# Regrouping results with VectorE blocks and on-chip transfers instead of TensorE transposes, in a two-layer encoder trunk

## The reference

```python
h = x                                            # (1, 256, 2048)
for i in range(2):
    u = rmsnorm(h, norm_mix[i])
    if i == 0:   # mixer A
        val, gate = split(u @ w_pw1 + b_pw1)     # 2048 -> 4096
        v = causal_depthwise_conv(val * sigmoid(gate), w_dw) + b_dw     # 31 taps
        m = silu(rmsnorm(v, g_norm)) @ w_pw2 + b_pw2
    else:        # mixer B
        gate_b, gate_c, v = split(u @ w_in)      # 2048 -> 6144
        m = (gate_b * causal_depthwise_conv(gate_c * v, w_conv3)) @ w_out
    h = h + m
    h = h + square(relu(rmsnorm(h, norm_mlp[i]) @ w1)) @ w2             # 2048 -> 8192 -> 2048
    h = h + sigmoid(rmsnorm(h, norm_ple[i]) @ w_gate) * (p[i] @ w_proj)
return rmsnorm(h, norm_final)
```

## Time and profile before

| what | value |
|---|---|
| median of three runs | 2347.74 us |
| profiled execution | 2345.66 us, span 2343.9 us |
| TensorE busy | 2317.7 us, 99% of the span |
| VectorE busy | 1407.9 us, 60% |
| ScalarE busy | 1000.7 us, 43% |
| transfers | 431.59 MB, mean 184 GB/s |
| the SP queue's packets | 54.9% of 16 engines' time |
| granted TensorE clock, mean | 0.998 |

### The profile page before, as it was taken

How to read it: one execution, slowest core, us unless ns; L and a number is a source line. 1 busy time by engine, 2 the same in 40 slices (tenths; PEclk the granted TensorE clock), 3 DMA queues, 4 the chain that set the end, 5 groups by cost and what they waited for, 6 DMA issues and landing times.

```text
span 2343.9 us, 31333 instructions
## 1 busy us (share of the span) xinstructions
PE 2317.7 (99%) x11258; PEld 1958.1 (84%) x11258; DVE 1407.9 (60%) x1761; ACT 1000.7 (43%) x1160; POOL 1.6 (0%) x9
## 2 busy tenths in 40 slices
PE   8999999999999999999999999999999999999997
PEld 6888678888888888888888888888888888888886
DVE  5999956555555555555656565556556556556565
ACT  2000445434444444455644444554344344344554
POOL 0000000000000000000000000000000000000000
PEclk9999999999999999999999999999999999999999
DMA  9444155555555555555555555555555555565553
GB/s 298 151 153 154 67 187 189 181 197 190 187 197 185 191 197 183 193 179 180 188 201 185 188 188 183 185 189 190 191 193 186 192 195 182 194 195 182 196 197 108
DMA packets 231282, 431.59 MB, mean 184 GB/s; under 512 B 7181, under 2 KB 40461, under 8 KB 230413
## 3 DMA queue, kind: packets, MB, share of 16 engines
q1 hardware_dynamic: 230448, 428.90, 54.9%
q10 hardware_dynamic: 632, 0.89, 0.1%
q0 software_dynamic: 144, 1.05, 0.1%
HBM read 428.70 MB, written 2.10 MB: 184 GB/s over the span
## 4 chain that ended last, share of the span: by engine, by line
PE 86%; issue 13%; DVE 0%; ACT 0%; DMA 0%; POOL 0%; DVEq 0%; POOLq 0%; ACTq 0%
PE acc L384 20%; PE acc L356 18%; PE acc L358 18%; PE acc L357 18%; PE acc L387 10%; PE acc L346 1%; PE acc L531 0%; PE acc L532 0%; PE acc L533 0%; DMA work<-in_cf_b_pw 0%; DVE wlo L820 0%; ACT L800 0%; DVE res L895 0%; DVE work L890 0%; DVE h L898 0%
## 5 line engine op out<-in xcount | busy, mean ns | idle before, releaser
L820 DVE TENSOR_TENSOR wlo<-raw,whi 128x1024 fp32r<-128x1024 f32 x732 | 885.9, 1223 | 726.0 <-ACT whi L552 717.4
L552 ACT ACTIVATE whi<-raw 128x1024 fp32r<-128x1024 f32 x732 | 769.8, 1059 | 853.9 <-PE acc L358 530.8
L356 PE MATMUL acc<-whi,both_b 128*128 128x512 f32 x1120 | 438.7, 392 | 1.9 <-DVE wlo L820 1.9
L358 PE MATMUL acc<-whi,both_b 128*128 128x512 f32 x1120 | 436.6, 390 | 0.0
L357 PE MATMUL acc<-wlo,both_b 128*128 128x512 f32 x1120 | 436.4, 390 | 0.0
L356 PE MATMUL acc<-whi,both_a 128*128 128x512 f32 x768 | 299.7, 390 | 0.0
L358 PE MATMUL acc<-whi,both_a 128*128 128x512 f32 x768 | 298.9, 389 | 0.0
L357 PE MATMUL acc<-wlo,both_a 128*128 128x512 f32 x768 | 298.9, 389 | 0.0
L384 PE MATMUL acc<-both_b,whi 128*128 128x512 f32 x1024 | 257.3, 392 | 0.0
L384 PE MATMUL acc<-both_a,whi 128*128 128x512 f32 x1024 | 257.3, 392 | 0.0
L356 PEld LDWEIGHTS acc<-whi,both_b 128*128 128x128 f32 x1120 | 210.7, 188 | 46.6 <-issue 2.6
(11 more groups left out here) (137 smaller groups left out, 1305.3 us busy)
## 6 DMA issues: line engine op xcount, KB each, us to landing
raw<-in_mlp_w SPq DMA_DIRECT2D x256, 1024.0 KB, 5.1
raw<-in_sc_w_in SPq DMA_DIRECT2D x48, 1024.0 KB, 5.2
raw<-in_cf_w_pw SPq DMA_DIRECT2D x64, 512.0 KB, 8.6
raw<-in_ple_w_gate SPq DMA_DIRECT2D x32, 1024.0 KB, 5.0
raw<-in_cf_w_pw SPq DMA_DIRECT2D x16, 1024.0 KB, 5.0
raw<-in_sc_w_out SPq DMA_DIRECT2D x16, 1024.0 KB, 5.0
wproj<-in_ple_w_proj SPq DMA_DIRECT2D x2, 2048.0 KB, 14.0
h<-in_x SPq DMA_DIRECT2D x4, 512.0 KB, 9.3
```

Source lines behind the costliest of these rows:

```text
L356: nc.tensor.matmul(o, xhi[:, k, s], hi, start=first and c == 0, stop=False)
L358: mm = nc.tensor.matmul(o, xlo[:, k, s], hi, start=False, stop=last and c == 1)
L552: nc.scalar.activation(whi[:, e % SLOTS, :, :], raw[:, e // 2, 2 * (e % 2):2 * (e % 2) + 2, :], ACT.Copy).then_inc(hi_ready, 1)
L820: nc.vector.tensor_tensor(wlo[:, e % SLOTS, :, :], raw[:, e // 2, 2 * (e % 2):2 * (e % 2) + 2, :], whi[:, e % SLOTS, :, :].bitcast(F32), A ...
```

## The change

1. **Turning.** The result `res` is turned by one VectorE instruction (`turn`, new) that transposes every 32 x 32 block by itself, into `turned`. The blocks then have to change partitions: SP issues 16 transfers (`move`, new), each from 32 partitions to 32 partitions, 32 KB in runs of 128 bytes, into `xt`. `operand_hi`, `operand_lo`, `to_vpad` and `short_out` read `xt` (in SBUF) and no longer PSUM. TensorE has no transposes left after the front.
2. **The MLP's up blocks** are computed by `multiply`, as all others are: the residual operand is held still, the weights are streamed. Their results come token by partition and so need turning too. ACT applies ReLU with the norm factor and the square; the down blocks' results are added without a factor. `NORM_MLP` becomes a full inverse root.
3. **Order.** `turn` and `add_gated` stand before DVE's split step e = 3. `move` stands in SP's list behind the first tile of a block, for the result of two blocks before that tile's block.
4. **Front.** Parameter rows are loaded 128 channels to a partition and turned by 6 transposes, ahead of the last piece of x; the squares and copies of x are shared between ACT and DVE, the norm no longer waits for the last copy; the 16 sums of squares on TensorE become additions on DVE (`add_squares`, new) and one product.

```diff
+            def move(T):
+                sp.wait_ge(tr_ready, T + 1)
+                for j in range(TILES):
+                    for i in range(TILES):
+                        nc.sync.dma_start(xt_parts[j * Q:(j + 1) * Q, :, i * Q:(i + 1) * Q],
+                                          turned[i * Q:(i + 1) * Q, 8 * j:8 * j + 8, :]).then_inc(xt_ready[j], 16)
...
-            def load(b, w, col, row=0):
+            def load(b, w, col, row=0, back=None):
                 for q in range(TILES):
                     tile(b, q, w[bass.ds(row + q * 4 * P, 4 * P), bass.ds(col, NB)]
                          .rearrange("(c r) n -> r c n", r=P))
+                    if q == 0 and back is not None:
+                        back()
...
+            def load_unit(unit, w, before, col=0, row=0):
+                for j in range(2):
+                    back = None if before is None else exchange(Result(before, BLOCKS - 2 + j))
+                    load(unit.b + j, w, j * NB + col, row, back)
+                with sp.Fori(2, BLOCKS) as j:
+                    load(unit.b + j, w, j * NB + col, row, exchange(Result(unit, j - 2)))
...
@@ TensorE @@
                     half(b, e, pair, xhi, xlo, (2 * e, 2 * e + 1), e == 0, e == HALVES - 1)
-                    if e == behind and pre is not None:
-                        pe.wait_ge(res_ready, pre[1] + 1)
-                        pe.wait_ge(tp_free, pre[0])
-                        transpose_group((c, m, res[:, m, c * P:(c + 1) * P])
-                                        for c in range(4) for m in range(2))
...
-                hidden_unit(up[0], BOTH[u], ready, before)
+                multiply_unit(up[0], X[u], ready)
...
@@ ScalarE @@
                 if r.kind == "hidden":
                     act.wait_ge(half_used, HALVES * r.b + HALVES)
                     act.wait_ge(acc_free, r.a)
-                    for p in range(2):
-                        nc.scalar.activation(side[:, 2 * p:2 * p + 2, :], acc[:, bass.ds(2 * r.pair + 4 * p, 2), 2 * P:4 * P],
-                                             ACT.Copy).then_inc(side_ready, 1)
+                    act.wait_ge(res_ready, r.t)
+                    for m in range(2):
+                        last = nc.scalar.activation(zb[:, m:m + 1, :], acc[:, bass.ds(2 * r.pair + m, 1), :],
+                                                    ACT.Relu, scale=rinv[:, m:m + 1])
+                    last.then_inc(acc_free, 1)
+                    act.wait_ge(acc_free, r.a + 1)
+                    act.wait_ge(tr_ready, r.T)
+                    nc.scalar.activation(res[:, :, :], zb, ACT.Square).then_inc(res_ready, 1)
...
-            def operand_hi(T, j, dst, gain=None, src=tp):
-                act.wait_ge(tp_done, T + 1)
+            def operand_hi(x, j, dst, gain=None):
+                for part in xt_ready:
+                    act.wait_ge(part, 64 * x + 64)
...
@@ VectorE @@
+            def turn(T, t):
+                dve.wait_ge(res_ready, t + 1)
+                for part in xt_ready:
+                    dve.wait_ge(part, 64 * T)
+                nc.vector.transpose(out=turned.rearrange("p (j k) t -> p j k t", j=TILES),
+                                    in_=res[:, :, :].rearrange("p m (c j f) -> p j (m c) f", j=TILES, c=4)
+                                    ).then_inc(tr_ready, 1)
...
             def run_behind(b, r, dst, gain=None, new_norm=None):
...
-                def between(e):
-                    if e == 3 and r.kind in ("gate", "gate_last"):
+                def before():
+                    process(r)
+                    if r.kind in ("gate", "gate_last"):
                         add_gated(r)
-                    if e == 4 and r.kind == "hidden":
-                        hidden_lo(r, dst)
-                run(b, lambda: process(r), after, between)
+                    if r.transposed:
+                        turn(r.T, r.t)
+                run(b, before, after)
...
+            def add_squares(n):
+                dve.wait_ge(sq_ready, n + 1)
+                if n:
+                    dve.wait_ge(sq_used, n)
+                    ins = nc.vector.tensor_tensor(sq_sum[:, :], sq_sum[:, :], sq[:, n % 4, :], ALU.add)
+                else:
+                    ins = nc.vector.tensor_copy(sq_sum[:, :], sq[:, 0, :])
+                ins.then_inc(sq_used, 1)
```

More of the change, by code:

```diff
@@ L299, in load_mlp, with load_win @@
                 by = distance(up[0], up[1])
-                with sp.Fori(0, GROUPS) as g:
-                    load_unit(up[0].shifted(by, g), w1, col=g * D)
-                    load_unit(down[0].shifted(by, g), w2, row=g * D)
+                load_unit(up[0], w1, before)
+                with sp.Fori(0, GROUPS - 1) as g:
+                    load_unit(down[0].shifted(by, g), w2, up[0].shifted(by, g), row=g * D)
+                    load_unit(up[1].shifted(by, g), w1, down[0].shifted(by, g), col=g * D + D)
+                load_unit(down[-1], w2, up[-1], row=GROUPS * D - D)
+            def load_win(next_j, product, gated):
+                for part, first, back in ((0, D, product), (1, 2 * D, gated), (2, 0, None)):
+                    load(win.b - 3 + 3 * next_j + part, t_in["sc_w_in"][0], next_j * NB + first - NB, back=back)
             def load_pair(u):
@@ L311, in load_pair @@
                                           .rearrange("(c r) n -> r c n", r=P)).then_inc(ready[ring][q], 16)
+            for j in range(TILES):
+                nc.sync.sem_inc(xt_ready[j], 64)
             for j in range(BLOCKS):
@@ L418, in multiply_mlp, with multiply_unit @@
-            def multiply_mlp(layer, u, ready, before):
+            def multiply_unit(unit, xin, ready, each=2):
+                multiply(unit.b, unit.a, 0, xin, ready, each)
+                with pe.Fori(1, BLOCKS) as j:
+                    multiply(unit.b + j, unit.a + j, j % 2, xin)
+            def multiply_mlp(layer, u, ready):
                 up, down = mlp[layer]
@@ L637, in after @@
                     if r.transposed:
-                        operand_hi(r.T, r.j, dst, gain)
-                    if new_norm is not None and new_norm != NORM_MLP:
+                        operand_hi(r.x, r.j, dst, gain)
+                    if new_norm is not None:
                         take_root(new_norm)
@@ L846, in process @@
             def process(r):
+                if r.kind in ("hidden", "gate", "gate_last"):
+                    return
                 product(r.b, r.a)
@@ L1000, in _ @@
             last.then_inc(diag_ready, 1)
+            x_copy(3)
             dve.wait_ge(spread_done, 1)
```

363 lines of the change are left out of this document (163 added, 200 removed).

## The result

The changed kernel takes 2461.43 us (median of 4 runs, 2450.76 to 2464.37), the kernel before 2347.64 us: a ratio of 1.0478, 95% interval [1.0454, 1.0503]. It is 4.8% slower; forecast were 2302 us and a range from 2288 to 2400.

The account below looks back on a forecast made before the run. TensorE, busy 99% of the span, was taken to bound the kernel: 2343.9 - 50.8 saved + 5 for waits and clock = 2298.1, +1.8 around it = 2300, runs 2.1 above the profiled one: 2302 us; range 2288 to 2400.

Parts of the forecast that it names:

- The step that failed: Regrouping of each result: SP issues a transfer in 0.373 us, so the last of 16 starts 5.6 us in.
- rival 2: Partial gain: issues of 0.5 us and a turning at half speed bring every `xt` 3.1 us later; 2330 us, chance 0.12.
- dues: Latest times in a block for an up result's `xt`: 13.9 us at a unit's start, 15.4 us inside a unit.
- break-even: Regrouping: at about 0.59 us per transfer, `xt` comes 3.3 us later and eats the 46 us of gain.
- Its zero: Time count in a block: 0 is TensorE's start of it; a w_pw2 result's sum starts at 0.2 us.
- the 12 us that it calls harmless: Blocks before the change: the high part starts 11.9 us after its block without TensorE waiting, taken as proof.
- Rival 1: Small runs are dear: at 352 packets per us a transfer takes 0.73 us; 2450 us, slower, chance 0.24.
- one fall: Granted clock falling after a TensorE wait at the gate: one such fall, costing 1.7 us.
- Front: Start of the kernel: sums off TensorE 5.6 us, earlier first norm 2.2 (bounds 0 and 3), 0.4 back; 7.4 us gained.
- Transposes: Blocks: 224 transposes leave TensorE, 28 groups of 0.88 us each, 24.6 us gained.
- Stationary form: MLP up blocks computed as down blocks: 32 blocks x 8 halves x 0.073 us, 18.8 us gained.
- The gate: Only late result: `xt` at 14.6 us, 0.4 us late in three blocks, 1.8 at the start of w_in.

Follow-up runs that it names:

- experiment 3: The changed kernel with its 16 transfers of 32 KB written in runs of 1 KB, not 128 bytes (words in another order): 2422.4 us, ratio 1.0321.
- experiment 4: No kernel work: transfers by themselves, 16 of each kind, from one engine or two at once; on-chip ones took SyncE 0.59 to 0.61 us to issue.
- experiment 1: The changed kernel without its transfers, operand parts read directly from the turned blocks (output not the reference's): 2292.42 us, ratio 0.9771.
- experiment 8: The kernel before with the new front and the MLP's up matmuls with the residual stationary, all results turned by TensorE: 2348.51 us, ratio 1.0003.
- experiment 7: The kernel before with the new front alone, all results still turned by TensorE: 2336.21 us, ratio 0.9957.
- experiment 5: The changed kernel with 8 of each result's 16 transfers issued by SyncE and 8 by GpSimd: 2316.14 us, ratio 0.9877.
- experiment 9: The changed kernel with 8 transfers on SyncE and 8 on GpSimd, GpSimd's issues as a loop, not written out: 2325.85 us, ratio 0.9909.
- experiment 10: The changed kernel with 10 transfers of each result on SyncE, 2 on GpSimd and 4 pieces copied by GpSimd: 2297.83 us, ratio 0.9791.

## Why the prediction was wrong

**The step that failed** is "SP needs 0.373 us to issue one; the last of 16 starts 5.6 us in". The row is right, but it is a 1 MB load from HBM. A 32 KB transfer from one place on chip to another takes 0.611 us, 0.654 from start to start; the last starts 9.8 us in. Experiments 3 and 4 show that neither bytes nor rows nor runs make it so. The prediction bounded the price of a run from both sides; for an issue it tried 0.5 us, in its range and in rival 2. Against that it held that 256 issues were within 0.01 us of 0.373, but those are all of one kind. The kernel before also loads x, in four transfers of 512 KB with another shape, and they cost more to issue:

```profile
L314 SPq DMA_DIRECT2D h<-in_x x4: 444/470/608, 0.8 to 2.3; - x4
```

So the trace before already showed that the price of an issue depends on the kind of transfer.

**The rest of its working carries the loss.** Put 0.654 into it: `xt` is 4.2 us later. Up results had 11.9; with 4.2, and 0.6 more that ACT and VectorE take ahead of the transfers, that is 16.7 (measured: 16.6) against dues of 13.9 at a unit's start and 15.4 inside. So 2.7 and 1.2 us late, in 8 and 24 blocks; measured there, TensorE's matmuls are mostly 2.4 and 1.4 us later than without a wait. The prediction had its break-even at 0.59 us a transfer, and 0.654 lies beyond.

**Its zero was off by a little.** It starts a w_pw2 result's sum 0.2 us into the block. In the kernel before

```profile
328.57 0.39 PE L356 MATMUL acc<-whi,both_b 128*128 128x512 f32 x1
```

is the block's first matmul (the second stands four halves, 10.9 us, behind the 317.89 of the earlier trace rows), and the sum starts at 329.29: 0.72 us in. An up result of the changed kernel is taken up 0.57 us in. The due times count from the first matmul, so every operand is some 0.4 us nearer to its due time than the prediction has it, and the 12 us that it calls harmless are 12.4. In the block shown above that makes 17.0 against 15.4, 1.6 us late, and 1.6 is what its matmul lost (1.82 us from start to start where 0.23 is normal); at a unit's start the same count gives 3.1, where mostly 2.4 is measured. This alone would not have turned the sign: with 0.4 us more than its own 11.9 the up results still meet 13.9.

**Rival 1 had nearly the right time, 2450 us, for a wrong reason.** It held that the queue hands out at most 352 packets per us, so 0.73 us a transfer. A run took 13 ns, the queue handed out 380 per us (3808 in 10) with its engines idle two thirds of the time, and with SyncE and ScalarE issuing at once it handed out 715:

```profile
q10 hardware_dynamic: 3613, 0.44, 26.6%
q1 hardware_dynamic: 3536, 0.43, 25.6%
```

(experiment 4, 149.5 to 159.5 us: 7149 packets in 10 us). The signal it named, issues stretched over 0.6 us, came true, but as the cost of an issue. The Trainium skill, "DMA: Bandwidth & Descriptors", section "Specifications", says that below 512 bytes a transfer is read, modified and written. No price that matters came of it here: 13 ns for a run of 128 bytes.

**The ledger**, by spans. Without the transfers: 2292.1 - 2343.9 = -51.8. With them: +169.5. Of that the first products' idle time is 62.7 + 60.1 - 3.1 = 119.7. The mean clock of 0.982 instead of 0.997 makes an estimated (0.018 x 2461.6) - (0.003 x 2292.1) = 37 us, for matmuls that run at a lower clock behind the gaps. The rest, 12 us, is mostly that each gap also hides 0.16 us behind a matmul's modelled end (1.82 us from start to start where 0.23 is normal, shown as 1.44 idle): some 60 gaps make 10. So the clock took nearly a third as much as the waits. The prediction had priced one fall, 1.7 us; it did not ask what repeated ones would cost.

**The gains came.** Predicted -50.8 and +5, measured -55.2 in the medians (experiment 1).
- Front: 7.4 forecast, 11.3 measured by itself (7 to 13). The first matmul of the blocks comes 10.3 us sooner, and the mis-sized term is the one that was given bounds of 0 and 3: the scaling of xT starts at 15.86 instead of 21.41 us, 5.6 us and not 2.2. The parameters' transposes now stand ahead of x's last piece and the norm ahead of its last copy; what each of the two gives was not run. The chunks give the other 4.8, forecast 5.2. In the changed kernel:

```profile
15.86 6.42 DVE L1005 SCALAR_TENSOR_TENSOR xT<-xT,vec_rows,ones_rb 128x256 f32<-128x256 f32 x16
269.39 0.80 PE L395 MATMUL acc<-whi,b_hi 128*128 128x512 f32 x1
```

  and the first block matmul before:

```profile
279.71 0.80 PE L356 MATMUL acc<-whi,both_b 128*128 128x512 f32 x1
```
- Transposes: experiments 8 and 1 differ by 60 groups and 56.1 us: 0.94 us each, forecast 0.88.
- Stationary form: experiments 7 and 8 differ by 32 more groups and 32 up blocks: 12.3 = 32 x (0.94 - g), so g = 0.55 us a block, forecast 0.587. The scatter of the medians leaves g uncertain by some 0.1 us, so both agree.
- Turning: 1.246 us, forecast 1.23. Landing 2.0, forecast 2.3. Runs under 22 ns, as taken.
- The gate was late as said, but TensorE idled 4.59 us in three blocks and 4.17 at the start of w_in, not 0.4 and 1.8.

**The Trainium skill.** "Perfetto Trace Analysis", section "What "DMA-bound" means", lists the issuing engine's sequencer as a bound of its own beside the DMA engines. The trace agrees: SyncE's issues lead the chain for 22% of the span, and while they run (586 to 596 us) the engines move data for 31% of the time. "DMA: Bandwidth & Descriptors", section "Issuing engines are not separate DMA queues", says that issuing from several engines saves only the time of the issue, which is usually small beside the transfer. Here it is the whole matter: half of the issues on another engine is worth 145 us (experiment 5). The section "Rules for kernel authors", which the prediction weighed and set aside because transfers overlap, would have been the safer guide; the overlap is real in landing (2.0 us) and absent in issue. Were the 50 ns that the section "Anatomy of one DMA — SWDGE (gpsimd) path" gives for the sequencer's dispatch all that an issue costs on GpSimd, 16 would be an estimated 0.8 us. Measured are 9.3 us (experiment 4, L115); for SyncE's 10.4 us that section has no figure.

**What stays open:** why a source on chip costs 0.16 us more to issue than one in HBM of the same shape, what GpSimd does every 60 transfers, and what makes it begin 0.35 us later in a loop.

## What to carry to other kernels

When a change adds many small transfers, count the issues in series on their engine and price them by a row of the same kind (source, destination and shape), or measure 16 in a row; where no such row exists, give that price bounds too. Where an operand has a due time, work out how the time moves per us of lateness: this kernel forgave about 6 us between the first issue and the last, and from 7.2 us on lost more than 50 us for one, lower clock included. A regrouping of this kind pays once its issues are spread over engines that have time: 10 on one, 2 and four plain copies on another turned 4.8% slower into 2.1% faster.

## What had not been expected of the hardware

- An on-chip transfer takes 0.59 to 0.61 us to issue on SyncE, from 4 to 32 KB; at 32 KB it is 0.63 on ScalarE and 0.58 on GpSimd. One of the same shape from HBM takes 0.45 on SyncE, a 1 MB tile 0.376 (experiment 4).
- SyncE and ScalarE, or SyncE and GpSimd, issue at the same time without slowing each other by more than 0.02 us an issue (experiment 4).
- A packet of 128 bytes on chip took 13 ns of a DMA engine (0.311 x 160 us / 3808).
- GpSimd stops for 2.8 us after every 60 of its transfers, in written-out code and in a loop alike (experiments 5 and 9); with 2 transfers a result instead of 8 it is again the 60th (experiment 10).
- VectorE turns 128 x 1024 words in 32 x 32 blocks in 1.246 us; an addition of that size takes 1.23.
